# Down projection of ten of eleven feed-forward steps per layer as seven block products in place of eight

## What is computed

```
x = x + concat(differential attention, latent attention) @ w_o
h = rms(x) * ffn_norm
x = x + (silu(h @ w_gate) * (h @ w_up)) @ w_down        # w_gate, w_up: 1024 x 2816; w_down: 2816 x 1024
```

## Time and profile before

| | us |
|---|---|
| time, median of 3 runs | 2489.72 (2488.95 to 2491.81) |
| the profiled execution's own time | 2487.16 |
| its span, first to last instruction | 2485.4 |
| PE busy in the span | 2408.0 |
| DVE busy | 1317.9 |
| POOL busy | 925.4 |
| ACT busy | 567.7 |

### The profile page before, as it was taken

The page is one execution under the profiler, slowest core; times in us unless marked ns, Lnnn a source line. Parts: engine busy times, 40 slices in busy tenths (PEclk is TensorE's granted clock), DMA queues, the critical chain, the costliest instruction groups (busy, mean ns, idle before and its releaser), DMA issues.

```text
span 2485.4 us, 31149 instructions
## 1 busy us (share of the span) xinstructions
PE 2408.0 (97%) x11304; PEld 1999.7 (80%) x11304; DVE 1317.9 (53%) x2369; ACT 567.7 (23%) x1095; POOL 925.4 (37%) x792
## 2 busy tenths in 40 slices
PE   7989999989999999999999999999999999999996
PEld 5777788868888888888888888877788888888885
DVE  6998488873333333333358865888433333333335
ACT  3445134520000000000124532454000000000001
POOL 6425200165666666665200010004544443344421
PEclk9999999999999999999999999999999999999998
DMA  8533431242333333332133134222211111111101
GB/s 307 174 102 127 178 136 68 102 144 93 120 114 112 120 124 127 127 127 68 51 121 117 59 133 179 96 89 107 68 51 51 43 50 42 51 51 51 51 17 68
DMA packets 50345, 249.52 MB, mean 100 GB/s; under 512 B 5968, under 2 KB 6096, under 8 KB 32720
## 3 DMA queue, kind: packets, MB, share of 16 engines
q1 hardware_dynamic: 49536, 247.52, 29.2%
q10 hardware_dynamic: 720, 0.86, 0.1%
HBM read 187.54 MB, written 60.82 MB: 100 GB/s over the span
## 4 chain that ended last, share of the span: by engine, by line
PE 86%; DVE 6%; POOL 1%; issue 1%; DMA 0%; ACT 0%; SPq 0%; DVEq 0%; POOLq 0%; ACTq 0%
PE bank L449 28%; PE bank L451 27%; PE bank L450 27%; PE bank L806 2%; PE bank L669 1%; POOL w L580 1%; POOL w L575 1%; PE bank L677 1%; DVE aT_lo L1380 1%; DVE qpe L1256 1%; DVE mx L1372 0%; DMA raw<-in_wffn 0%; PE bank L456 0%; PE bank L455 0%; DVE ms L1199 0%
## 5 line engine op out<-in xcount | busy, mean ns | idle before, releaser
L449 PE MATMUL bank<-h_hi,w 128*128 128x512 f32 x1792 | 704.8, 393 | 7.3 <-issue 6.3
L451 PE MATMUL bank<-h_hi,w 128*128 128x512 f32 x1792 | 700.0, 391 | 0.0
L450 PE MATMUL bank<-h_lo,w 128*128 128x512 f32 x1792 | 699.9, 391 | 0.0
L575 POOL TENSOR_TENSOR w<-raw,zero 128x512 fp32r<-128x512 f32 x312 | 329.3, 1076 | 785.5 <-PE bank L451 725.1
L580 POOL TENSOR_TENSOR w<-raw,w 128x512 fp32r<-128x512 f32 x318 | 413.2, 1320 | 24.7 <-ACT w L1058 12.4
L449 PEld LDWEIGHTS bank<-h_hi,w 128*128 128x128 f32 x1792 | 338.4, 189 | 77.6 <-issue 8.5
L451 PEld LDWEIGHTS bank<-h_hi,w 128*128 128x128 f32 x1792 | 337.9, 189 | 71.4
L450 PEld LDWEIGHTS bank<-h_lo,w 128*128 128x128 f32 x1792 | 338.3, 189 | 69.2
L1423 DVE TENSOR_TENSOR x<-x,bank 128x512 f32<-128x512 f32 x352 | 239.8, 686 | 187.3 <-PE bank L451 184.3
L449 PE MATMUL bank<-u_hi,w 128*128 128x512 f32 x704 | 273.9, 389 | 0.0
L450 PE MATMUL bank<-u_lo,w 128*128 128x512 f32 x704 | 273.9, 389 | 0.0
(11 more groups left out here) (163 smaller groups left out, 3329.4 us busy)
## 6 DMA issues: line engine op xcount, KB each, us to landing
w<-parked SPq DMA_DIRECT2D x81, 1024.0 KB, 4.8
raw<-in_wffn SPq DMA_DIRECT2D x132, 512.0 KB, 3.5
parked<-w SPq DMA_DIRECT2D x27, 1024.0 KB, 6.6
parked<-p SPq DMA_DIRECT2D x27, 1024.0 KB, 4.8
raw<-in_watt SPq DMA_DIRECT2D x27, 512.0 KB, 4.6
praw<-in_watt SPq DMA_DIRECT2D x27, 512.0 KB, 5.7
out_yT<-y_out SPq DMA_DIRECT2D x16, 256.0 KB, 2.3
x<-in_xT SPq DMA_DIRECT2D x4, 512.0 KB, 6.8
```

Of the source, the lines that this page charges most:

```text
L449: nc.tensor.matmul(out_ap, lhs[0], rhs[0], start=first, stop=False)
L450: nc.tensor.matmul(out_ap, lhs[0], rhs[1], start=False, stop=False)
L451: return nc.tensor.matmul(out_ap, lhs[1], rhs[0], start=False, stop=last)
L575: last = nc.gpsimd.tensor_tensor(w[slot][0][:, cols], src[:, cols], zeros_like(src[:, cols]), ALU.add)
```

## The change

In steps 0 to 9 of each layer (`SEVEN` = 10) the down projection of both requests is one 2 x 2 block product: its rows are the two halves of the output features (A11, A12 over A21, A22; columns are the two hidden blocks of the step), its columns the two requests (B11, B12 over B21, B22, the four gated blocks). It is computed in Winograd's form, with seven products of half size:

- weight sums, on GpSimd: S1 = A21 + A22, S2 = S1 - A11, S3 = A11 - A21, and -S4 = S2 - A12, made in place in the raw buffers and `a_sum`
- operand sums, on VectorE: T1 = B12 - B11, T2 = B22 - T1, T3 = B22 - B12, T4 = T2 - B21, made in `silu`, `t_sum`, `u_other`
- P1 = A11 B11, P2 = A12 B21, P3 = S4 B22 (made with the sign turned, N3), P4 = A22 T4, P5 = S1 T1, P6 = S2 T2, P7 = S3 T3, of 12 matmuls each (four quarters of three passes)

Each of the seven factors on either side is split into hi (now ScalarE for the weights too) and lo (GpSimd for weights, VectorE for operands). The sum of products over the steps can be kept back: VectorE adds each product, over all ten steps, to one or two of four places and forms the outputs from these once. Those places are x's own buffer. So x itself is stored to DRAM (`x_kept`, 2 MB for each request) and the first product to reach a place overwrites it. The eleventh step is as before, with the down weights split by ScalarE and GpSimd, and in it VectorE undoes the sums and adds x back, four rows of 256 KB at a time, from one buffer (`x_back`) that is loaded again when it has been used.

TensorE's order in a step becomes: gate and up 0; P7 and P6 of the step before; gate and up 1; P1; gate and up 2; P5; gate and up 3; P2, N3, P4. P7, P6, P1, P5, P2 and P4 use the banks 4 to 7; N3 uses 0 to 3, the banks of gate and up. The rope tables, whose place is used for a raw buffer, are loaded again for layer 1.

```diff
-FMM = 8 + 2 * KT
-FCHUNK_FREE = [2, 3, 6, 7, FMM - 1, FMM - 1]
+FMM = 8
+FCHUNK_FREE = [2, 3, 6, 7]
+SEVEN = FC - 1
+MH = KT // 2
+P1, P5, P2, N3, P4, P7, P6 = [MH * n for n in range(7)]
+NPROD = 7 * MH
+A1, A5, A2, B3, A4, A7, A6 = [MH * n for n in (0, 2, 4, 5, 7, 8, 9)]
+NACC = 10 * MH
...
+            def load_back(l, m):
+                if m:
+                    sp.wait_ge(s_back.sem, s_back.layer_at(l, 6 * m - 1))
...
+                for b in range(B):
+                    for k in range(2):
+                        sp.dma_start(x_back[:, b, k, :], x_kept[:, b, k * MH + m, :]).then_inc(s_x_back, 16)
...
+            def seven_step(l, c, first, last, prep):          # SP
+                if not first:
+                    load_down(l, c, 1)
+                    load_down(l, c, 0)
+                if prep:
+                    prep_next(prep_at(c, 0))
+                    prep_next(prep_at(c, 1))
+                load_raw(l, c + 1, 2)
+                load_raw(l, c + 1, 3)
+                if prep:
+                    prep_next(prep_at(c, 2))
+                if not last:
+                    load_raw(l, c + 2, 0)
+                    load_raw(l, c + 2, 1)
...
+            def seven_step(l, c, preps):                      # GpSimd
+                a11, a21 = [down_raw[0][:, cols] for cols in spans(2)]
+                a12 = down_raw[1][:, 0:CH // 2]
+                down_lo(l, c, 0)
+                pool.wait_ge(s_down_raw[1], 16 * (l * FC + 1) + c * 16)
+                a22 = down_raw[1][:, CH // 2:CH]
+                nc.gpsimd.tensor_tensor(a_sum[:], a21, a22, ALU.add).then_inc(s_a_sum.sem, 1)
+                nc.gpsimd.tensor_tensor(a21, a11, a21, ALU.subtract).then_inc(s_a_sum.sem, 1)
+                pool.wait_ge(s_a_sum.sem, s_a_sum.step_at(l, c, 0))
+                nc.gpsimd.tensor_tensor(a11, a_sum[:], a11, ALU.subtract).then_inc(s_a_sum.sem, 1)
+                if preps:
+                    prep(prep_at(c, 0))
+                    prep(prep_at(c, 1))
+                down_lo(l, c, 1)
+                down_lo(l, c, 2)
+                pool.wait_ge(s_a_sum.sem, s_a_sum.step_at(l, c, 2))
+                nc.gpsimd.tensor_tensor(a12, a11, a12, ALU.subtract).then_inc(s_a_sum.sem, 1)
+                down_lo(l, c, 3)
+                next_split(l, c, 0)
+                next_split(l, c, 1)
+                down_lo(l, c, 4)
+                if preps:
+                    prep(prep_at(c, 2))
+                down_lo(l, c, 5)
+                next_split(l, c, 2)
+                next_split(l, c, 3)
+                down_lo(l, c, 6)
...
+            def gate_up(l, c, ev, first):                     # TensorE
...
+                    if ev >= 2:
+                        last_read = s_silu if part == 0 else s_gated
+                        pe.wait_ge(last_read.sem, last_read.step_at(l, c, ev - 2))
+                    elif not first:
+                        pe.wait_ge(s_acc.sem, s_acc.step_at(l, c, B3 + 2 * (2 * part + ev) + 1 - NACC))
...
+            def products_234(l, c):
+
+                pe.wait_ge(s_a_lo.sem, s_a_lo.step_at(l, c, 2))
+                pe.wait_ge(s_u_lo.sem, s_u_lo.step_at(l, c, 2))
+                for m in range(MH):
+                    pe.wait_ge(s_acc.sem, s_acc.step_at(l, c, A5 + 2 * m + 1))
+                    quarter(2, operand_slot(2), m, 4 + m)
+
+                pe.wait_ge(s_a_lo.sem, s_a_lo.step_at(l, c, 3))
+                pe.wait_ge(s_u_lo.sem, s_u_lo.step_at(l, c, 3))
+                for m in range(MH):
+                    last_read = s_silu if m < 2 else s_gated
+                    pe.wait_ge(last_read.sem, last_read.step_at(l, c, 2 + m % 2))
+                    quarter(3, operand_slot(3), m, m)
+
+                pe.wait_ge(s_a_lo.sem, s_a_lo.step_at(l, c, 4))
+                pe.wait_ge(s_u_lo.sem, s_u_lo.step_at(l, c, 4))
+                for m in range(MH):
+                    pe.wait_ge(s_acc.sem, s_acc.step_at(l, c, A2 + m))
+                    quarter(0, operand_slot(4), m, 4 + m)
+
+            def products_76(l, c):
...
+                for m in range(MH):
+                    pe.wait_ge(s_acc.sem, s_acc.step_at(l, c, A7 + m - NACC))
+                    quarter(2, operand_slot(5), m, 4 + m)
...
+                def seven_step(c, first):                     # ScalarE
+                    before = (s_mm.sem, s_mm.half_at(l, 1, NMM - 1))
+                    down_hi(c, 0, raw_down(c, 0), before if first else prod(c, P4 - NPROD))
...
+                    silu_of(c, 0, True)
+                    moving_hi(c, 0, gated(c, 0), None if first else P4 + MH - 1 - NPROD)
+                    down_hi(c, 1, weights_summed(c, 0), before if first else prod(c, P7 - NPROD))
+                    down_hi(c, 2, raw_down(c, 1), before if first else prod(c, P6 - NPROD))
+                    down_hi(c, 3, weights_summed(c, 3), before if first else prod(c, N3 - NPROD))
+                    silu_of(c, 1, True)
...
+                def gated(c, ev, out):                        # VectorE
+                    zg, zu = bank[ev % 2], bank[2 + ev % 2]
+                    dve.wait_ge(s_mm.sem, s_mm.step_at(l, c, 2 * ev))
+                    nc.vector.tensor_tensor(zg[:], zg[:], scaled[:, ev % 2, :], ALU.mult).then_inc(s_gate.sem, 1)
+                    dve.wait_ge(s_silu.sem, s_silu.step_at(l, c, ev))
+                    nc.vector.tensor_tensor(silu[ev % 2][:], silu[ev % 2][:], scaled[:, ev % 2, :], ALU.mult).then_inc(s_up.sem, 1)
+                    dve.wait_ge(s_mm.sem, s_mm.step_at(l, c, 2 * ev + 1))
+                    dve.wait_ge(s_up.sem, s_up.step_at(l, c, ev))
+                    nc.vector.tensor_tensor(out[:], zu[:], silu[ev % 2][:], ALU.mult).then_inc(s_gated.sem, 1)
...
+                def seven_step(c, first):
+                    gated(c, 0, silu[0])
+                    moving_lo(c, 0)
+                    if not first:
+                        previous(c)
+
+                    gated(c, 1, u_other)
+                    dve.wait_ge(s_gated.sem, s_gated.step_at(l, c, 1))
+                    moving_sum(t_sum, u_other, silu[0])
+                    moving_lo(c, 1)
...
+                    for m in range(MH):
+                        add_products(c, P1, 4, m, c12, ALU.add, first)
+                        add_products(c, P1, 4, m, c11, ALU.add, first)
+                    gated(c, 2, silu[0])
+                    moving_lo(c, 2)
+                    dve.wait_ge(s_acc.sem, s_acc.step_at(l, c, A5 - 1))
+                    for m in range(MH):
+                        add_products(c, P5, 4, m, c12, ALU.add)
+                        add_products(c, P5, 4, m, d3, ALU.add, first)
+                    gated(c, 3, silu[1])
+
+                    dve.wait_ge(s_gated.sem, s_gated.step_at(l, c, 3))
+                    moving_sum(t_sum, silu[1], t_sum)
+                    moving_lo(c, 3)
+                    dve.wait_ge(s_t_sum.sem, s_t_sum.step_at(l, c, 1))
+                    moving_sum(silu[0], t_sum, silu[0])
+                    moving_lo(c, 4)
+                    dve.wait_ge(s_acc.sem, s_acc.step_at(l, c, A2 - 1))
+                    for m in range(MH):
+                        add_products(c, P2, 4, m, c11, ALU.add)
+                    for m in range(MH):
+                        add_products(c, N3, 0, m, c12, ALU.subtract)
+                        add_products(c, N3, 0, m, d2, ALU.add, first)
+                    for m in range(MH):
+                        add_products(c, P4, 4, m, d3, ALU.add)
+                    moving_sum(u_other, silu[1], u_other)
+                    moving_lo(c, 5)
+                    moving_lo(c, 6)
...
+                seven_step(0, True)
+                with dve.Fori(1, SEVEN) as c:
+                    seven_step(c, False)
+                for ev in range(4):
+                    gated(SEVEN, ev, silu[ev % 2])
...
+                    if ev == 0:
+                        previous(SEVEN)
+                        dve.wait_ge(s_acc.sem, s_acc.step_at(l, SEVEN - 1, NACC - 1))
+                    elif ev < 3:
+                        sums_undone(2 * ev - 2)
+                        sums_undone(2 * ev - 1)
```

More of the change, by code:

```diff
@@ L240, with prep_at @@
 PREP_STEPS = 9
-def prep_at(c, j):
-    return (c - 1) * 3 + j // 2 if 1 <= c <= PREP_STEPS and j % 2 == 0 else None
+def prep_at(c, n):
+    return 3 * c + n if c < PREP_STEPS else None
 def encoder_trunk(nc, xT, watt, wffn, tables, gains, lam, out):
@@ L827, in apply_values @@
                 last.then_inc(s_av.sem, 1)
[L829 to L853, removed]
-                                               [hb[s][:, k, :] for s in range(2)], k == 0, k == KT - 1)
-                            last.then_inc(s_mm.sem, 1)
-                            if first and ev == 0 and part == 1:
-                                norm_sums("last", l)
-                            if first and ev == 1 and part == 0:
-                                norm_spread("last", l)
@@ new lines, in quarter, with product_1 @@
```

(53 more changed lines are left out.)

320 lines of the change are left out of this document (239 added, 81 removed).

## The result

The kernel with the change takes 2573.76 us (median of 4 runs, 2570.14 to 2574.41) against 2489.34 us, a ratio of 1.0331 (95% interval 1.0318 to 1.0344): 84 us slower. The forecast was 2594, with 0.85 on slower. The profiled execution took 2574.41 us, its span is 2572.6.

A forecast was written before the change was run, and what follows sets the result against it. PE alone was taken to set the FFN's time. Stalls of 64 us (layer 1), 92 (layer 0) and 4 (clock), 160 in all, minus 54.4 saved gave +105: forecast 2594 us, range 2505 to 2635.

The forecast's parts named there:

- What PE saves: Down projection, 20 steps: seven products of 12 matmuls replace eight, 240 matmuls fewer, -54.4 us.
- Place A: End of a step: POOL's split blocks DVE's two-SBUF instructions, delaying N3, P4 and the next gate; stall 2.85 us.
- Place B: P7 and P6 in the next step: P6 waits for P7's banks behind late DVE adds; stall 2.7 us.
- table load: ACT before silu, one kept in each loop body: 1.28 us.
- Layer 0: POOL also prepares layer 1's weights in nine steps and waits for loads; such a step 71.3 us, 6.0 more than before.
- The wait before P5: Layer-0 steps: late silu 1 delays P1's adds, so P5 ends at 58.8, not 57.2: 1.55 us.
- the late last gated block: Layer-0 steps: P2's and P5's adds pass the delay on; the product opening place A is 1.6 us late.
- Last steps: Last step of each layer: first down add waits for DVE's undone groups and their loads; stall 8.4 us a layer.
- 1 (port free): Places A and B: DVE finds the port free, stalls 0.55 and 0.1 to 1.4; 2475 us; 0.15 together with break-even.
- 2 (half clock): P6's wait in each of 20 steps also costs clock, 1.3 us each, +27: 2621 us; 0.15 with other overruns.
- 3: Layer 0: the chain is hidden after all, by quicker load or POOL less behind, -28: 2566 us; 0.25 with milder stalls.
- 4: Seven products not issued in all 20 steps, or gate products take more matmuls; chance 2 in 100.

The follow-up runs named there:

- experiment 6: Changed kernel with the edits of experiments 5, 1 and 3, and both next-step down-chunk loads ahead of the last raw chunk: 2445.33 us, ratio 0.9822.
- experiment 1: Changed kernel with POOL's split of the step's last up chunk moved behind the remainder of the S2 weights: 2567.20 us, ratio 1.0311.
- 7: Kernel of experiment 6 with the last up chunk's split put back ahead of the S2 remainder, and experiment 2's load order: 2490.56 us, ratio 1.0007.
- 8: Kernel of experiment 6 with six write-only POOL memsets added at the end of each layer-1 step: 2444.22 us, ratio 0.9814.
- 9: Kernel of experiment 6 with five SBUF-reading POOL copies added at the end of each layer-1 step: 2466.19 us, ratio 0.9897.
- experiment 5: Changed kernel with POOL's second preparation behind S4's remainder and the third's load asked for earlier on SP, in nine layer-0 steps: 2513.51 us, ratio 1.0102.
- Experiment 3: Changed kernel with one undone group after each gated block of the eleventh step, instead of two after the second and third: 2552.08 us, ratio 1.0252.
- experiment 2: Changed kernel with the next step's second down chunk loaded before the gate and up chunks of the step after, on SP: 2558.78 us, ratio 1.0277.

## Why the prediction was right, and where it was off

- **What PE saves.** 240 matmuls, 54 us: exact in the count. With most waits out of the way (experiment 6) 44 to 46 of it arrive.
- **Place A.** Right in mechanism, place and price: remainders at 3.27 and 6.66 us against 3.3 and 6.8. PE's loss was 2.2 and not 2.85 us (the next gate product started 10.3 after the last up product, not 11.0), mostly because I priced adds at their duration. Experiments 1, 7, 8 and 9 show the cause.
- **Place B.** Mis-sized in layer 1: 0.9 in place of 2.7 us. Sixteen adds took 1.4 us less, and there was no table load: `ACT_TABLE_LOAD` before silu is x2 where it was x22, one a layer. I had kept one in each loop body, though I saw that the body now begins with a copy; that the copy is the reason was not tested. These two sizes, 10 x (0.65 + 1.8) = 24.5 us, are about all by which layer 1 was forecast too slow: +39 with the clock, against 11.1 behind its first step and 5.4 ahead of it, 22 less.
- **Layer 0.** A step of 71.3 was forecast and 71.5 to 72.1 measured, but the parts were other ones. The wait before P5 (forecast 1.55) was not there, and the late last gated block cost 0.4 (forecast 1.6). Place A cost 2.3 apart from that (forecast 2.85). Place B cost 4.85 where I had 2.7: the prediction let the first down chunk land before it was needed and did not see that SP asks for it behind the last split and beside three other transfers. The half clock behind that wait adds some 1.6. That it came out right in the sum is luck in good part: the layer's path led through the first down chunk and P6, not through silu 1 and P5. That POOL's waits for praw are behind it is what the prediction said, and experiment 5 showed it at 60 us.
- **Last steps.** PE waited 10.1 and 9.0 us, forecast 8.4, and the clock was at half behind them, as forecast. Experiment 3 confirmed the cause.
- **Rivals.** 1 (port free) fell in the changed kernel; experiment 6 made it free and came out at 2445, below the 2475 that I gave it. 2 (half clock) was true in layer 0 only, where waits are 4.6 us and more. 3 was true of the chain that it named, from silu 1 to P5, but the wait before P6 stood in its place and layer 0 was no faster. 4 fell by the count.
- What stays open: no run tests what is left before P6 in the best kernel (0.6 to 0.7 us a step), nor what decides the clock behind waits of 2 to 3 us (last section).

## What to carry to other kernels

Fewer matmuls only pay when each engine's written order still hands PE its operands and banks in time: count, at each place where PE reuses a bank, what stands ahead of the freeing instruction on its engine. A copy or a load request that stands ahead of an urgent instruction in an in-order queue is the urgent instruction's price, and moving two lines (experiment 5) was worth 60 us here. Keep POOL work that reads SBUF away from short chains of DVE instructions with two SBUF operands: in this kernel one split at the wrong moment cost 2.4 us in each of 20 steps.

## What the runs showed of the hardware that I had not expected

- Independent DVE instructions back to back had a pace of 0.60 us with a recorded duration of 0.68 to 0.69 (16 adds in 9.64 us).
- POOL's memsets did not slow DVE at all (0.685 us), POOL's copies made the same instruction 1.525; the loss on POOL's side was about 0.4 us for each DVE instruction let in.
- A wait of 4.6 us was enough for half clock (0.57 over the 3 us behind it), one of 0.6 was not (1.00). In between, the length of the one wait does not decide. Behind 2.28 us idle before P6 in layer 0 of experiment 2 the clock was 0.50, behind 2.46 us before P6 in layer 1 of experiment 1 it stayed 1.00:

```profile
825.60:828.60 3.00, 3.00 (x7) 2.42 (x8) 2.41 (x5) 0.00 (x0) 2.92 (x4) 0.50 0.00 0
```
```profile
1958.40:1961.40 3.00, 3.00 (x13) 2.48 (x14) 3.00 (x6) 0.01 (x1) 1.67 (x2) 1.00 0.00 0
```

  So the waits of 2.7 us that the prediction had before P6 could have gone either way.
